# The first two weight units behind each inner norm of a hybrid decoder step, run ahead of the norm's root

## The reference, cut to what matters

```python
def _rmsnorm(x, g):
    y = x32 * lax.rsqrt(jnp.mean(x32 * x32, axis=-1, keepdims=True) + EPS)
    return y * g
def _modulate(xn, shift, scale):
    return xn * (1.0 + scale[:, None, :]) + shift[:, None, :]
mod = jax.nn.silu(c) @ p['ada_w'] + p['ada_b']
sh1, sc1, g1, sh2, sc2, g2, sh3, sc3, g3 = jnp.split(mod, N_MOD, axis=-1)
u = _modulate(_rmsnorm(x, p['norm_ff1']), sh1, sc1)
x = x + 0.5 * g1 * _swiglu(u, ff1_w1, ff1_w3, ff1_w2)
u = _modulate(_rmsnorm(x, p['norm_mix']), sh2, sc2)     # inner norm 1
... = _split_cols(u @ p['w_in'])                        # mixer: mLSTM and SSD branches
x = x + g2 * (merged @ p['w_out'])
u = _modulate(_rmsnorm(x, p['norm_ff2']), sh3, sc3)     # inner norm 2
x = x + 0.5 * g3 * _swiglu(u, ff2_w1, ff2_w3, ff2_w2)
```

## Time and profile before

| | us |
|---|---|
| median of 3 runs | 1318.34 |
| lowest, highest | 1318.19, 1320.57 |
| span of the profiled execution | 1321.6 |
| PE busy in it | 1265.6 |
| DVE, ACT, POOL busy | 767.1, 618.3, 206.4 |

### The profile page before, as it was taken

The page is one execution under the profiler, slowest core; times in us unless marked ns, Lnnn a source line. Parts: engine busy times, 40 slices in busy tenths (PEclk is TensorE's granted clock), DMA queues, the critical chain, the costliest instruction groups (busy, mean ns, idle before and its releaser), DMA issues. The chain is left out here.

```text
span 1321.6 us, 22659 instructions
## 1 busy us (share of the span) xinstructions
PE 1265.6 (96%) x9096; PEld 1153.0 (87%) x9096; DVE 767.1 (58%) x1326; ACT 618.3 (47%) x1070; POOL 206.4 (16%) x377
## 2 busy tenths in 40 slices
PE   6899999998999899999999999999999999999997
PEld 3699999997997777778998888888989979999997
DVE  0744445435795456865378877865476565555433
ACT  3433334333757646645355665554653343333342
POOL 4100000000550312211023322221500010000010
PEclk9899999998999999999999999999999999999998
DMA  9857777776333679885674365464436554553551
GB/s 288 257 177 238 222 227 219 212 216 217 124 107 106 220 262 345 301 281 143 188 203 129 108 207 161 135 201 131 143 87 171 177 182 152 157 158 118 146 152 41
DMA packets 258862, 241.56 MB, mean 183 GB/s; under 512 B 8607, under 2 KB 242479, under 8 KB 258710
## 3 DMA queue, kind: packets, MB, share of 16 engines
q1 hardware_dynamic: 249262, 211.03, 52.4%
q0 software_dynamic: 9024, 28.91, 6.4%
q10 hardware_dynamic: 472, 0.17, 0.1%
...
## 5 line engine op out<-in xcount | busy, mean ns | idle before, releaser
L2159 DVE TENSOR_TENSOR w_lo<-ring,w_hi 128x1024 fp32r<-128x1024 f32 (+1 forms) x264 | 336.6, 1276 | 413.0 <-ACT w_hi L1580 412.2
L1580 ACT ACTIVATE w_hi<-ring 128x1024 fp32r<-128x1024 f32 (+1 forms) x264 | 289.3, 1097 | 508.8 <-PE bank L865 504.0
L865 PE MATMUL bank<-u_hi,w_hi 128*128 128x320 f32 x1536 | 274.1, 321 | 10.3 <-ACT u_hi L1605 5.1
L865 PEld LDWEIGHTS bank<-u_hi,w_hi 128*128 128x128 f32 x1536 | 236.0, 191 | 29.1 <-issue 19.6
L865 PE MATMUL bank<-u_hi,w_lo 128*128 128x320 f32 x1536 | 256.3, 309 | 0.3 <-DVE w_lo L2159 0.2
L865 PE MATMUL bank<-u_lo,w_hi 128*128 128x320 f32 x1536 | 256.5, 309 | 0.0
L865 PEld LDWEIGHTS bank<-u_lo,w_hi 128*128 128x128 f32 x1536 | 233.9, 188 | 0.0
L865 PEld LDWEIGHTS bank<-u_hi,w_lo 128*128 128x128 f32 x1536 | 232.9, 188 | 0.9 <-DVE w_lo L2159 0.8
L661 POOL TENSOR_TENSOR arena<-arena 128x320 f32<-128x320 f32 x24 | 21.0, 873 | 610.6 <-ACT arena L1592 597.8
L862 PE MATMUL aux<-ident,arena 128*128 128x128 f32 (+6 forms) x404 | 63.3, 283 | 17.4 <-ACT arena L1637 8.8
L862 PEld LDWEIGHTS aux<-ident,arena 128*128 128x128 f32 (+6 forms) x404 | 45.3, 145 | 31.8 <-issue 17.1
...
## 6 DMA issues: line engine op xcount, KB each, us to landing
ring<-in_w_in SPq DMA_DIRECT2D x52, 1024.0 KB, 5.4
ring<-in_ff_w SPq DMA_DIRECT2D x44, 1024.0 KB, 5.5
ring<-in_ada_w SPq DMA_DIRECT2D x36, 1024.0 KB, 7.6
...
ring<-in_w_pa SPq DMA_DIRECT2D x8, 1024.0 KB, 8.1
...
```

Source lines behind the costliest of these rows:

```text
L865: return nc.tensor.matmul(dst, lhs, rhs, start=first, stop=last)
L1580: nc.scalar.activation(w_hi[v.split_no % 2][:, 0:v.kc, :], panel_part(v), ACT.Copy).then_inc(S["hi_done"], 1)
L2159: V.tensor_tensor(w_lo[r][:, 0:v.kc, :], panel_part(v), w_hi[r][:, 0:v.kc, :].bitcast(FP32), ALU.subtract)\
```

## The change

The first two units behind each gap (qk 0 and 1, up2 0 and 1) are no longer fed from the normed activations. They take x times the scale column, split into high and low parts tile by tile while the stage before the gap still runs (`gained_high` on ACT, `gained_low` on DVE, samples by POOL). Their outputs are multiplied by the inverse root afterwards, and a product of shift and weights is added: PE forms it from the raw panel (`shift_rows`, 16 instructions like an adaLN unit), ACT copies it out, PE turns it, DVE sums it (`bias_cols`), ACT and DVE add it (`early_scaled`, `early_shifted`). The panel of these two units moves ahead of the three adaLN panels in the load order, the adaLN units move behind the two units, and `dense_two` now runs units 2 and 3 from the normed activations. The sample part of the norm moves from DVE to POOL. The gate matmuls and what hangs on them move from behind unit 1 to behind unit 3, and each of their steps one or two units later. Several semaphores are merged under new names. The core of the diff, with twelve leading blanks taken off where a line had them:

```diff
-ROWS_BEFORE = (0, 12, 21)
-TILES_BEFORE = (0, 9, 18)
+ROWS_BEFORE = (0, 20, 37)
+TILES_BEFORE = (0, 8, 16)
...
+EARLY = {name: [(name, 0), (name, 1)] for name in ("qk", "up2")}
...
-    order += [("ada", a) for a in ADA_GAP2]
-    order += [("qk", q) for q in range(16)] + list(ROW_UNITS) + [u for head in HEAD_UNITS for u in head]
+    order += EARLY["qk"] + [("ada", a) for a in ADA_GAP2]
+    order += [("qk", q) for q in range(2, 16)] + list(ROW_UNITS) + [u for head in HEAD_UNITS for u in head]
...
-    order += [("ada", a) for a in ADA_GAP3]
-    order += [("up2", q) for q in range(2 * KF)]
+    order += EARLY["up2"] + [("ada", a) for a in ADA_GAP3]
+    order += [("up2", q) for q in range(2, 2 * KF)]
...
+    if left is not None and (left.name, left.q) in (("qk", 1), ("up2", 1)):
+        sp_.wait_ge(S["shift_mm"], shift_at(1 if left.name == "qk" else 2, 1))
...
+def gained_samples(n):
+    for kc in range(KD):
+        pool.wait_ge(S["res_done"], before_gap(n, kc))
+        nc.gpsimd.tensor_tensor(sequences(xg_s[n][:, kc, :]), sequences(x_t[:, kc, TP:T]),
+                                gain[:, kc, 1:NSEQ].unsqueeze(2).to_broadcast([128, SB, ST]), ALU.mult).then_inc(S["us_ready"], 1)
+        if 1 <= kc < KD - 1:
+            pool.wait_ge(S["sq_ready"], n * KD + kc + 1)
+            ins = nc.gpsimd.tensor_tensor(sq[:, 0, :], sq[:, 0, :], sq[:, kc, :], ALU.add)
+            if kc < KD - 2:
+                ch.link(ins)
+            else:
+                ins.then_inc(S["sq_summed"], 1)
+def normed_samples(n, shift):
+    pool.wait_ge(S["inverse_ready"], inverse_at(n, 0))
+    pool.wait_ge(S["u_lo_ready"], gained_at(n, KD - 1))
+    ch.link(nc.gpsimd.tensor_tensor(xg_s[n][:, :, :], xg_s[n][:, :, :], rs[:, None, TP:T].to_broadcast([128, KD, TS]), ALU.mult))
+    nc.gpsimd.tensor_tensor(u_t[:, :, TP:T].rearrange("p k (b t) -> p k b t", t=ST), xg_s[n][:, :, :].rearrange("p k (b t) -> p k b t", t=ST),
+                            mod[:, shift * KD:(shift + 1) * KD, 1:NSEQ].unsqueeze(3).to_broadcast([128, KD, SB, ST]), ALU.add).then_inc(S["us_ready"], 1)
 sum_of_squares(0)
 first_samples()
-sum_of_squares(1)
-samples(1)
+gained_samples(1)
+normed_samples(1, 3)
...
+    if (u.name, u.q) in EARLY["qk"]:
+        pool.wait_ge(S["early_put"], early_at(1, 2 + u.q))
...
+def shift_rows(n, shift, u):
+    pe.wait_ge(slot_in[u.slot], u.arrivals)
+    pe.wait_ge(S["mod_read"], 4 * shift + 8)
+    if n == 2:
+        pe.wait_ge(S["early_made"], early_at(1, 1))
+    w, columns = panel_dst(u), mod[:, :, :].rearrange("p q s -> p (q s)")
+    for kc in range(KD):
+        g, first = kc % 4, NSEQ * (shift * KD + kc)
+        ins = mm(aux[1][32 * g:32 * g + 32, 0:256], columns[:, first:first + 32], w[:, kc, :], kc < 4, kc >= 4)
+    ins.then_inc(S["shift_mm"], 1)
+def shift_columns(n):
+    pe.wait_ge(S["early_put"], early_at(n, 1))
+    for j in range(2):
+        ins = turn(aux[1][:, 256 + j * 128:384 + j * 128], bias_row[:, j * 128:(j + 1) * 128], 128)
+    ins.then_inc(S["shift_mm"], 1)
+def dense_early(u, n):
+    bank, r, high, low = bank_of(u), u.split_no % 2, gained_hi[n], gained_lo[n]
+    if u.uses:
+        pe.wait_ge(bank_free[u.bank], u.uses)
+    pe.wait_ge(S["hi_done"], u.split_no + 1)
+    for kc in range(KD - 1):
+        pe.wait_ge(S["u_hi_ready"], gained_at(n, kc))
+        mm(bank, w_hi[r][:, kc, :], high[:, kc, :], kc == 0, False)
+    sum_squares_most(n)
+    sum_squares_last(n)
+    for kc in range(KD - 1):
+        pe.wait_ge(S["u_lo_ready"], gained_at(n, kc))
+        mm(bank, w_hi[r][:, kc, :], low[:, kc, :], False, False)
+    pe.wait_ge(S["lo_done"], u.split_no + 1)
+    for kc in range(KD - 1):
+        mm(bank, w_lo[r][:, kc, :], high[:, kc, :], False, False)
+    kc = KD - 1
+    pe.wait_ge(S["u_hi_ready"], gained_at(n, kc))
+    mm(bank, w_hi[r][:, kc, :], high[:, kc, :], False, False)
+    mm(bank, w_lo[r][:, kc, :], high[:, kc, :], False, False)
+    pe.wait_ge(S["u_lo_ready"], gained_at(n, kc))
+    mm(bank, w_hi[r][:, kc, :], low[:, kc, :], False, True).then_inc(unit_done, 1)
+def early_units(n, shift, name, fill):
+    shift_rows(n, shift, st.at[name, 0])
+    dense_early(st.at[name, 0], n)
+    shift_columns(n)
+    dense(st.at[name, 1], gained_hi[n], gained_lo[n])
+    for a in fill:
+        ada(a)
+    mod_columns(fill[0])
+    dense_two((st.at[name, 2], st.at[name, 3]), n)
+    mod_columns(fill[1])
+    mod_columns(fill[2])
...
-sum_squares_most(1)
-for u in st.range(("ada", ADA_GAP2[0]), ("ada", ADA_GAP2[-1])):
-    ada(u)
-    if before and before.name == "ada":
-        mod_columns(before)
-    if u.q == ADA_GAP2[0]:
-        sum_squares_last(1)
-    before = u
+if before.name == "ada":
+    mod_columns(before)
+early_units(1, 3, "qk", [st.at["ada", a] for a in ADA_GAP2])
...
-    if u.q == 0:
-        dense_two((u, st.at["qk", 1]), 1)
-    elif u.q > 1:
+    if u.q > 3:
         dense(u)
-    if u.q == 1:
-        mod_columns(before)
+    if u.q == 3:
+        pe.wait_ge(S["early_made"], early_at(1, 1))
         for kc in range(KD):
             mm(aux[1][0:40, 0:T], gate_hi[:, kc, :], u_hi[:, kc, :], kc == 0, False)
             mm(aux[1][0:40, 0:T], gate_hi[:, kc, :], u_lo[:, kc, :], False, False)
             ins = mm(aux[1][0:40, 0:T], gate_lo[:, kc, :], u_hi[:, kc, :], False, kc == KD - 1)
-        ins.then_inc(S["gate_mm"], 1)
-    if u.q == 2:
+        ins.then_inc(S["gates_mm"], 1)
+    if u.q == 4:
...
-def norm_high(n, shift):
-    act.wait_ge(S["xr_ready"], TILES_BEFORE[n])
+def gained_high(n, kc):
+    nc.scalar.activation(gained_hi[n][:, kc, 0:TP], x_t[:, kc, 0:TP], ACT.Copy, scale=gain[:, kc, 0:1])
+    act.wait_ge(S["us_ready"], samples_at(n, kc))
+    copy(gained_hi[n][:, kc, TP:T], xg_s[n][:, kc, :]).then_inc(S["u_hi_ready"], 1)
+def early_shifted(n, u):
+    act.wait_ge(S["early_made"], early_at(n, 2 + u.q))
+    shift = bias_cols[:, u.q, 0:1]
+    if u.name == "qk":
+        row = pad[:, u.q, HIST:HIST + TP]
+        nc.scalar.activation(row, row, ACT.Identity, bias=shift).then_inc(S["early_put"], 1)
+        return
+    nc.scalar.activation(ff_a[:, u.q, 0:TP], ff_a[:, u.q, 0:TP], ACT.Silu, bias=shift)
+    nc.scalar.activation(ff_a[:, u.q, TP:T], ff_a[:, u.q, TP:T], ACT.Silu).then_inc(S["early_put"], 1)
+def gap(n, shift, name, fill):
+    us = [st.at[name, q] for q in range(4)]
+    high_ahead(us[0], us[1])
+    act.wait_ge(S["shift_mm"], shift_at(n, 1))
+    copy(bias_row, aux[1][:, 0:256]).then_inc(S["early_put"], 1)
+    root(n)
+    high_ahead(us[0], us[2])
+    act.wait_ge(S["us_ready"], samples_at(n, KD))
     copy(u_hi[:, :, TP:T], u_t[:, :, TP:T]).then_inc(S["u_hi_ready"], 1)
     for kc in range(KD):
         tile_high(n, shift, kc)
+        if kc == 0:
+            early_shifted(n, us[0])
+        if kc == 3:
+            ada_row(fill[0])
+            high_ahead(us[1], us[3])
+    ada_row(fill[1])
+    early_shifted(n, us[1])
+    ada_row(fill[2])
...
+    if u.own >= 2:
+        conv(u, pad, 4)
     if u.own > 0:
         conv_silu(st.at["qk", u.own - 1], acc, qk_t)
...
+def gained_low(n, kc):
+    dve.wait_ge(S["u_hi_ready"], gained_at(n, kc))
+    hi, lo = gained_hi[n], gained_lo[n]
+    ch.inc(V.scalar_tensor_tensor(out=lo[:, kc, 0:TP], in0=x_t[:, kc, 0:TP], scalar=gain[:, kc, 0:1], in1=hi[:, kc, 0:TP].bitcast(FP32),
+                                  op0=ALU.mult, op1=ALU.subtract))
+    V.tensor_tensor(lo[:, kc, TP:T], xg_s[n][:, kc, :], hi[:, kc, TP:T].bitcast(FP32), ALU.subtract).then_inc(S["u_lo_ready"], 1)
...
+def early_scaled(n, u):
+    dve.wait_ge(unit_done, u.done)
+    x = banks[u.bank]
+    if u.name == "qk":
+        prompt, samples = pad[:, u.q, HIST:HIST + TP], pad[:, u.q, HIST + TP:].rearrange("p (b w) -> p b w", w=HIST + ST)[:, :, HIST:]
+    else:
+        prompt, samples = ff_a[:, u.q, 0:TP], sequences(ff_a[:, u.q, TP:T])
+    ch.inc(V.tensor_tensor(prompt, x[:, 0:TP], rs[:, 0:TP], ALU.mult))
+    V.tensor_tensor(samples, sequences(x[:, TP:T]), sequences(rs[:, TP:T]), ALU.mult).then_inc(bank_free[u.bank], 1)
+    dve.wait_ge(bank_free[u.bank], u.freed)
+    V.tensor_tensor(samples, samples, bias_cols[:, u.q, 1:NSEQ].unsqueeze(2).to_broadcast([128, SB, ST]), ALU.add).then_inc(S["early_made"], 1)
+def gap_norm(n, shift, name, fill):
+    us = [st.at[name, q] for q in range(4)]
+    gained_low(n, KD - 1)
+    low_ahead(us[0], us[1])
     dve.wait_ge(S["root_ready"], n + 1)
-    ch.link(V.reciprocal(rs[:, TP:T], rs[:, TP:T]))
-    dve.wait_ge(S["us_ready"], 4 + n)
-    ch.link(V.tensor_tensor(xg_s[:, :, :], xg_s[:, :, :], rs[:, None, TP:T].to_broadcast([128, KD, TS]), ALU.mult))
-    V.tensor_tensor(u_t[:, :, TP:T].rearrange("p k (b t) -> p k b t", t=ST), xg_s[:, :, :].rearrange("p k (b t) -> p k b t", t=ST),
-                    mod_of(shift)[:, :, 1:NSEQ].unsqueeze(3).to_broadcast([128, KD, SB, ST]), ALU.add).then_inc(S["xr_ready"], 1)
+    V.reciprocal(rs[:, TP:T], rs[:, TP:T]).then_inc(S["inverse_ready"], 1)
```

(84 more changed lines are left out.)

66 lines of the change are left out of this document (30 added, 36 removed).

## The result

The changed kernel takes 1323.72 us (median of 20 runs, 1321.05 to 1326.15), the kernel before 1319.99 in the runs beside them (20 runs, 1318.11 to 1325.53): ratio **1.0026, 95% interval 1.0019 to 1.0033**, 3.4 us slower. The forecast was 1316.3, with a range up to 1320.5.

What follows compares the result with a forecast made beforehand. PE, busy 1265.6 of 1321.6 us, was taken to bound the kernel by its own order. Gap 1 at -2.7 and gap 2 at +0.7 gave -2.0 us from the median 1318.34, so 1316.3, range 1313.2 to 1320.5.

Steps and rivals of the forecast that it cites:

- The out loop, costed at nothing on PE: In out, ACT's cycle grows to about 4.0 us against PE's 3.52; the copies' lead covers the slide, so PE loses 0.
- that rival (1 us through late copies): In out, POOL's product at 0.57 us or slower makes copies for units 6 and 7 late: about 1 us, 1317.3; chance 0.12.
- Gap 1, forecast at -2.7: Between down1 and qk: qk unit 5 starts at 343.9 instead of 346.59, a win of 2.7 us.
- Gap 2, forecast at +0.7: Between out and up2: PE waits 2.5 and 1.5 us; up2 unit 4 starts at 1091.6 against 1090.90, losing 0.7 us.
- the clock rival: Both gaps: lowered clock falls over dense units; +3.6 us, 1321.9, or 1319.1 at half, 3.4 us low each; chance 0.18.
- The marks: PE's starts of qk unit 5 (346.59) and up2 unit 4 (1090.90) in the profiled execution, taken to hold the change's whole effect.
- The verdict "no change": Whole kernel: time within about 0.2%, 2.6 us, of the kernel before; chance 0.49.
- "slower": Whole kernel: slower by over 0.2%, taking most of the case of a badly placed lowered clock; chance 0.15.
- The rival in which the waits don't reach PE: Both gaps: knock-on waits and table load stay hidden, 1.4 us more in gap 1, 1.3 in gap 2: 1313.6; chance 0.28.

Runs made afterwards that it cites:

- after_again: The changed kernel run a second time, unchanged, to see where its clock falls; its profiled execution took 1322.95 us.
- before_third: The kernel before, run a third time, unchanged, to see where its clock falls; its profiled execution took 1320.89 us.
- before_again: The kernel before, run a second time, unchanged, to see where its clock falls; ratio 1.0000, profiled execution 1325.96 us.
- row32_first: Against the changed kernel, ACT copies the adaLN row in out ahead of the square and the gained tile; ratio 0.9992 to the kernel before.
- filled_idle: Against the changed kernel, PE runs matmuls that nobody reads where it stands idle in both gaps; ratio 1.0010 to the kernel before.
- gap1_only: Against the changed kernel, only the gap between down1 and qk keeps the early units, the other is as before; ratio 1.0012 to the kernel before.
- gap2_only: Against the changed kernel, only the gap between out and up2 keeps the early units, the other is as before; ratio 1.0012 to the kernel before.
- silu_last: Against the changed kernel, unit 0's early output (with gap 2's table load) moves behind the eight normed tiles on ACT; ratio 1.0000 to the kernel before.

## Why the prediction was wrong

By the traces: +1.7 in out, -0.8 in gap 1 and +0.6 in gap 2 (means of changed and after_again, against the trace of before_third), +1.6 in the mixer, -0.6 elsewhere: +2.6 before rounding, where the medians say 3.4 with an uncertainty of 0.9. Against before_again, with its two stretches in the mixer, the same sum would be -0.7; before_third is taken because its clock is that of most executions.

1. **The out loop, costed at nothing on PE: the step that failed.** The cycle of ACT was forecast at 4.0 and is 4.05. I asked only whether the weight copies' lead covers the slide, and it does. What I left out is the adaLN row, which has no such lead: before, it stood behind the square alone, and PE had it 0.4 us early. Now it comes 2.0 us later against PE, 1.5 by the cycles of 4.05 ahead of it and 0.5 by the gained tile, and PE waits 1.50 us. row32_first takes the wait away. POOL's sample product, 0.445 us in the mean and 0.53 in most of out, was not the cause; that rival (1 us through late copies) had the right stage and the wrong mechanism.
2. **Gap 1, forecast at -2.7, came to -1.1.** The order was right nearly to the instruction: the panel holds ACT until 319.82 + 1.74 = 321.56 (forecast 321.75), PE turns at 325.4 (325.8), the waits behind it are 0.65 and 1.26 (0.3 and 1.1). The term that was mis-sized is the clock: 12 matmuls in 3.96 us instead of 2.78, the next 16 in 2.71 instead of 2.51, together 1.4. filled_idle gives it back and shows gap 1 at -2.6, and gap1_only, whose trace has no lowered stretch there, shows -2.5: without the clock's part the chain of the forecast was right.
3. **Gap 2, forecast at +0.7, came to +1.2 and 0.0.** Waits of 2.01 and 1.85 against 2.5 and 1.5; filled_idle and gap2_only, without the clock's part, have -0.1, 0.8 below the forecast: PE started unit 0 about 0.5 us sooner than I had it. The rest is where 3.4 us at 0.50 fall. The mechanism is in the clock rival with its right price (3.4 us in each gap, +2.8 to the forecast); what failed is its chance, 0.18. I took low stretches as lying where PE waits for tiles; in a gap where PE no longer waits for tiles they lie over dense work. That activity lifts the clock and idling lowers it (the Trainium skill, TensorE: Matmul & The Clock Gate, What's actually happening) agrees with filled_idle.
4. **The mixer, not in the sum at all.** I took PE behind qk unit 5 as the same in both kernels. A stretch of 1.6 us appears there in some executions of before and in all ten traces of changed kernels in which nothing is filled there. The idle places that it follows (1.83 us at 442, 2.14 at 711, 1.48 at 972) stand in before too; only the one at 359 (silu_last, filled_idle) is new. Filling them removes it. All 20 executions of the changed kernel have a granted clock of 0.990 or 0.991, the same as most of before, though gap 1 has 3.4 us less at 0.50, and that fits a stretch elsewhere in each of them. Why it comes more often behind a changed gap is open. The idle place at 359 is a wait of 1.1 us for the log decays, which were moved a unit later; no term of my sum had it, and it is regained by the place where PE of before waits at 404.6.
5. **The base.** The marks stood in an execution 3.4 us above its median. That alone moves nothing in a difference; but one trace gave me one set of lowered stretches, and I read their place as fixed.

The verdict "no change" at 0.49 and "slower" at 0.15 came from points 1 and 3. The rival in which the waits don't reach PE is refuted: all four were there.
